# First norm and attention projection in one stage by quarters, and attention unrolled with fewer instructions a head

## The reference, cut to what matters

```python
h = rms_norm(x, g_mix)                    # x: 2048 tokens x 1024
proj = h @ w_in                           # 1792 columns for the recurrence, 512 q, 128 k, 128 v
q, k = rms_norm over 64 dims of each head (q_gain, k_gain)      # 8 q heads, 2 kv heads
s = q @ k.T * 64 ** -0.5                  # each block of 128 queries against 384 keys
s = where(valid, s + bias, -inf)          # bias by distance, |distance| <= 128
m = maximum(max(s), sink)                 # one sink logit a head
pr = exp(s - m)
o = (pr / (sum(pr) + exp(sink - m))) @ v
x = x + concat(rwkv(proj), o) @ w_out
x = x + conv_glu(rms_norm(x, g_ffn))
```

## Time and profile before

| | |
|---|---|
| median of 3 runs | 3601.62 us (3600.74 to 3607.77) |
| the profiled execution | 3603.11 us, of which span 3601.3 us |
| PE busy | 3110.9 us, 86% of the span |
| DVE, ACT, POOL busy | 1673.6, 1176.5, 473.4 us |
| mean granted TensorE clock | 0.94 |

### The profile page before, as it was taken

How to read it: one execution, slowest core, us unless ns; L and a number is a source line. 1 busy time by engine, 2 the same in 40 slices (tenths; PEclk the granted TensorE clock), 3 DMA queues, 4 the chain that set the end, 5 groups by cost and what they waited for, 6 DMA issues and landing times. The chain is left out here.

```text
span 3601.3 us, 66272 instructions
## 1 busy us (share of the span) xinstructions
PE 3110.9 (86%) x27436; PEld 2532.8 (70%) x27436; DVE 1673.6 (46%) x2214; ACT 1176.5 (33%) x2240; POOL 473.4 (13%) x724
## 2 busy tenths in 40 slices
PE   3797888997562999999469859999999999799999
PEld 1575666886332999899237638888888888688887
DVE  3666773333454555543455564444444444333333
ACT  3335552112442444444233332222222222122222
POOL 0000000000326666561310000000000000000000
PEclk7899999998785999999789979999999999899999
DMA  4000002322355333321743101111111111522231
GB/s 121 24 12 27 15 15 62 70 70 66 115 217 176 103 108 113 101 62 33 225 154 117 70 18 47 47 52 47 47 47 47 47 47 47 199 90 82 93 96 35
DMA packets 185054, 284.69 MB, mean 79 GB/s; under 512 B 60009, under 2 KB 126953, under 8 KB 180234
## 3 DMA queue, kind: packets, MB, share of 16 engines
q1 hardware_dynamic: 183402, 280.41, 24.0%
q10 hardware_dynamic: 1440, 1.18, 0.1%
HBM read 185.09 MB, written 96.47 MB: 78 GB/s over the span
## 5 line engine op out<-in xcount | busy, mean ns | idle before, releaser
L164 PE MATMUL up_p<-h_hi,up_w_hi 128*128 128x512 f32 x1408 | 548.6, 390 | 26.6 <-DVE up_w_lo L1851 26.6
L165 PE MATMUL up_p<-h_lo,up_w_hi 128*128 128x512 f32 x1408 | 548.4, 390 | 0.0
L166 PE MATMUL up_p<-h_hi,up_w_lo 128*128 128x512 f32 x1408 | 548.4, 390 | 0.0
L1838 ACT COPY up_raw<-up_p 128x512 f32<-128x512 f32 x176 | 103.3, 587 | 718.6 <-PE up_p L166 718.6
L164 PEld LDWEIGHTS up_p<-h_hi,up_w_hi 128*128 128x128 f32 x1408 | 264.8, 188 | 82.5 <-issue 27.4
L1866 DVE TENSOR_SCALAR up_con<-up_raw,vecs_sb 128x2048 f32<-128x2048 f32 x44 | 59.3, 1347 | 539.7 <-ACT up_raw L1838 539.7
L165 PEld LDWEIGHTS up_p<-h_lo,up_w_hi 128*128 128x128 f32 x1408 | 264.7, 188 | 55.2
L166 PEld LDWEIGHTS up_p<-h_hi,up_w_lo 128*128 128x128 f32 x1408 | 264.7, 188 | 54.9
L164 PE MATMUL down_p<-down_act_hi,down_w_hi 128*128 128x512 f32 x704 | 274.7, 390 | 23.5 <-DVE down_act_lo L1991 23.5
L165 PE MATMUL down_p<-down_act_lo,down_w_hi 128*128 128x512 f32 x704 | 274.6, 390 | 0.0
L166 PE MATMUL down_p<-down_act_hi,down_w_lo 128*128 128x512 f32 x704 | 274.5, 390 | 0.0
(11 more groups left out here) (230 smaller groups left out, 6476.7 us busy)
## 6 DMA issues: line engine op xcount, KB each, us to landing
rec_inp<-gate_chunks SPq DMA_DIRECT2D x64, 512.0 KB, 3.5
up_w<-in_w_up SPq DMA_DIRECT2D x44, 512.0 KB, 3.4
act_out<-up_con SPq DMA_DIRECT2D x22, 1024.0 KB, 4.3
down_act<-act_out SPq DMA_DIRECT2D x88, 256.0 KB, 3.2
gate_chunks<-gates_out SPq DMA_DIRECT2D x4, 4096.0 KB, 11.9
rkv_chunks<-rwkv_project_mix SPq DMA_DIRECT2D x12, 1024.0 KB, 6.5
down_w<-in_w_down SPq DMA_DIRECT2D x22, 512.0 KB, 13.5
gate_chunks<-gates_out SPq DMA_DIRECT2D x4, 2048.0 KB, 7.1
```

Of the source, the lines that this page charges most:

```text
L164: pe.matmul(out, w_hi, x_hi, start=start, stop=False)
L165: pe.matmul(out, w_hi, x_lo, start=False, stop=False)
L166: return pe.matmul(out, w_lo, x_hi, start=False, stop=stop)
L1838: nc.scalar.copy(raw[:, half, 1 + n * NT:1 + (n + 1) * NT], p_u[:, half, n]).then_inc(S["copied_" + c], 1)
```

## The change

`start_block` and `attn_project_block` become `first_block`. It goes over 24 items g: quarter n = g // 6, column tile m = g % 6. Each item loads and splits its own weights again, 24 times instead of 6, ACT casting all 1024 columns at once and POOL subtracting. x has one buffer; the norm of quarter n + 1 is spread over the items of quarter n: squares at m = 1 and 2, root and reciprocal at m = 3, POOL's scaling in place at m = 3 and 4, high and low parts (with the gain, from the scaled tile) at m = 4 and 5. Normalised q is multiplied by -1/8 and stored to HBM (`q_dram`); k stays in SBUF. The bias row is negated, so scores and bias have their signs turned.

`attention_block` is unrolled over all 128 heads of blocks. q comes back from HBM. A score contracts the 64 rows of its kv head. One DVE instruction adds the bias and takes the minimum with the negated sink. The exponential has scale -1 and one more column, which holds the sink, so its sum is the whole denominator. POOL scales the probabilities by the reciprocal; the transposed tiles are copied by ACT and DVE in turn; weighing takes v as weights and the probabilities as moving data and writes channels on partitions, so the output transpose and the division are gone. The stages of a head lie up to 11 heads apart.

```diff
+            def _(sp):                                  # first_block
+                def load_x(n, ks):
+                    for k in ks:
+                        done(sp, "low", (n - 1) * KD + k + 1)
+                        sp.dma_start(xt[:, k], K.d["xT"][:, k, toks(n)]).then_inc(S[f"x_in{k}"], 16)
+                def load_w(g):
+                    done(sp, "w_lo", g)
+                    sp.dma_start(w[:, :, :], K.d["w_attn"][g % MT]).then_inc(S["w_in"], 16)
...
+                load_w(0)
+                sp.wait_ge(S["bias_copied"], 1)
+                sp.dma_start(K.bias_rows, row.unsqueeze(1).to_broadcast([AH, P, 512])).then_inc(
+                    S["bias_out"], 16)
+                def body(g, n, m):
+                    if g + 1 < ITEMS:
+                        load_w(g + 1)
+                    if m == 0 and n + 1 < TN:
+                        load_x(n + 1, range(KD))
+                    if m >= 1 and is_qk(g - 1) and m - 1 < QK - 1:
+                        q = g - 1
+                        done(sp, "normed", qk_count(q) + 1)
+                        sp.dma_start(K.q_dram[:, m - 1, toks(n)], raw[:, q % 2]).then_inc(
+                            S[f"q_saved{q % 2}"], 16)
+            def _(pe):
+                def body(g, n, m):
+                    done(pe, "w_lo", g + 1)
+                    done(pe, "copied", g - 1)
...
+                    for k in range(KD):
+                        if m == 0:
+                            done(pe, "low", n * KD + k + 1)
+                        mm = product(pe, p_proj[:, g % 2], w_hi[:, g % 2, k], w_lo[:, g % 2, k],
+                                     K.h_hi[:, k, toks(n)], K.h_lo[:, k, toks(n)], k == 0, k == KD - 1)
+                    mm.then_inc(S["projected"], 1)
+                    if g >= 1:
+                        heads(g - 1) if is_qk(g - 1) else turn_v(g - 1)
+                    if n + 1 < TN and m in (1, 2):
+                        squares(n + 1, range(4 * (m - 1), 4 * m))
+            def _(act):
+                def take(g):
+                    done(act, "projected", g + 1)
...
+                    if g == 0 or g == 1:
+                        done(act, "bias_out", 16)
...
+                def body(g, n, m):
+                    if g + 1 < ITEMS:
+                        split(g + 1)
+                    if g >= 1:
+                        head_root(g - 1) if is_qk(g - 1) else copy_v(g - 1)
+                    if n + 1 < TN:
+                        if m in (1, 2):
+                            squares(n + 1, range(4 * (m - 1), 4 * m))
+                        elif m == 3:
+                            root(n + 1)
+                        elif m >= 4:
+                            high(n + 1, range(4 * (m - 4), 4 * (m - 3)))
+                    take(g)
+            def _(pool):
+                def body(g, n, m):
+                    if g + 1 < ITEMS:
+                        split(g + 1)
+                    if n + 1 < TN and m in (3, 4):
+                        scale(n + 1, range(4 * (m - 3), 4 * (m - 2)))
+            def _(dve):
+                def body(g, n, m):
+                    if g >= 1 and is_qk(g - 1):
+                        normed(g - 1)
+                    if n + 1 < TN:
+                        if m == 3:
+                            invert(n + 1)
+                        elif m >= 4:
+                            low(n + 1, range(4 * (m - 4), 4 * (m - 3)))
...
+    PB = 12                                             # attention_block
+    TURN, WEIGH = 8, 10
...
+                    rows = slice(HD * (h // HH), HD * (h // HH) + HD)
+                    done(pe, "biased", i - 2)
...
-                    pe.matmul(p_s[:, h % 2, lo:hi], q_heads[:, h, :],
-                              K.qk[:, AH // 2, bass.ds(b * P - P + lo, hi - lo)], start=True,
+                    pe.matmul(p_s[:, i % 3, lo:hi], q[rows, b % 2, h % HH],
+                              K.k_t[rows, b * P - P + lo:b * P - P + hi], start=True,
...
-                        mm = pe.matmul(p_o[:, j, h % HH, :], prob_t[:, h % 2, c, :], v,
+                    out = p_o[HD * (h % 2):HD * (h % 2) + HD, b % 2, h // 2]
+                        mm = pe.matmul(out, K.v_tok[:, b - 1 + c, HD * j:HD * j + HD], prob_t[:, i % 4, c],
...
+                slots(pe, (0, score), (TURN, turn), (WEIGH, weigh))
+                    nc.scalar.activation(prob[:, i % PB, lo:hi + 1], s_sb[:, h, lo:hi + 1], ACT.Exp, scale=-1.0,
+                                         bias=least[:, b % 2, h:h + 1],
+                                         accum_out=den[:, b % 2, h:h + 1]).then_inc(S["exped"], 1)
+                slots(act, (1, exp), (TURN + 1, copy), (WEIGH + 1, copy_out))
+                    nc.gpsimd.tensor_scalar(prob[:, i % PB, lo:hi], prob[:, i % PB, lo:hi],
+                                            inv[:, b % 2, h:h + 1], None, ALU.mult).then_inc(S["scaled"], 1)
+                slots(pool, (5, scale))
+                    nc.vector.tensor_tensor_reduce(
+                        s_sb[:, h, lo:hi], p_s[:, i % 3, lo:hi], bias[:, h, lo:hi], 1.0, nsink[:, h:h + 1],
+                        ALU.add, ALU.min, least[:, b % 2, h:h + 1]).then_inc(S["biased"], 1)
+                slots(dve, (0, score), (2, invert), (TURN + 1, copy))
```

More of the change, by code:

```diff
@@ L204, in _ @@
+                sp.dma_start(outside, K.d["outside"]).then_inc(S["rb_in"], 16)
                 sp.dma_start(relb[:, :], K.d["rel_bias"]).then_inc(S["rb_in"], 16)
[L205 to L214, removed]
@@ L217, in _, with squares @@
             @block.scalar
             def _(act):
[L219 to L228, removed]
+                def squares(n, ks):
+                    for k in ks:
+                        done(act, f"x_in{k}", 16 * (n + 1))
+                        done(act, "x_summed", n * KD + k - 1)
+                        nc.scalar.activation(sq[:, k % 2], xt[:, k], ACT.Square).then_inc(S["x_squared"], 1)
@@ new lines, in _ @@
+                act.wait_ge(S["const_in"], 32)
+                squares(0, range(KD))
+                root(0)
+                split(0)
+                high(0, range(KD))
+                def body(g, n, m):
[11 more added lines that the diff above has]
+                    take(g)
@@ L383, in attention_block @@
     HH = AH // 2
+    W = 3 * P
+    ITEMS = NB * AH
+    PB = 12
+    TURN, WEIGH = 8, 10
     with ExitStack() as ctx:
@@ L406, in window @@
         def window(b):
-            end = isinstance(b, int)
-            return (P if end and b == 0 else 0, 2 * P if end and b == NB - 1 else 3 * P)
-        def has(b):
-            return not isinstance(b, int) or b >= 0
-        def wait(eng, name, value):
-            if not isinstance(value, int) or value > 0:
-                eng.wait_ge(S[name], value)
-        def item(b, h):
-            return (b, h) if h >= 0 else (b - 1, h + AH)
-        def blocks(eng, body):
-            body(0)
-            body(1)
-            with eng.Fori(2, NB - 1) as b:
-                body(b)
-            body(NB - 1)
+            return (P if b == 0 else 0, 2 * P if b == NB - 1 else W)
@@ L430, in attention_block, with done, copied, slots @@
+        def done(eng, name, n):
+            if n > 0:
+                eng.wait_ge(S[name], n)
+        def copied(eng, i):
+            if i >= 0:
+                done(eng, "copied_odd" if i % 2 else "copied_even", i // 2 + 1)
+        def slots(eng, *stages):
+            last = max(lag for lag, _ in stages)
+            for i in range(ITEMS + last):
+                for lag, stage in stages:
+                    if 0 <= i - lag < ITEMS:
+                        stage(*items[i - lag])
         with nc.Block() as block:
@@ L489, in slot @@
-                def slot(b, h, scores=True):
-                    if scores:
-                        score(b, h)
-                    for lag, stage in ((2, turn), (3, weigh)):
-                        if has(item(b, h - lag)[0]) and (scores or h - lag < 0):
-                            stage(*item(b, h - lag))
-                    if h == 5 and has(b - 1):
-                        turn_out(b - 1)
-                blocks(pe, lambda b: [slot(b, h) for h in range(AH)])
-                for h in (0, 1, 2, 5):
-                    slot(NB, h, False)
+                slots(pe, (0, score), (TURN, turn), (WEIGH, weigh))
```

531 lines of the change are left out of this document (244 added, 287 removed).

## The result

The changed kernel takes **3850.2 us** (median of 4 runs, 3845.3 to 3855.8), the kernel before 3604.7 beside it (4 runs): a ratio of 1.068, 95% interval 1.066 to 1.070. It is 6.8% slower, where the forecast was 3574 in a range of 3545 to 3640. The profiled execution took 3855.8 us, its span 3854.0.

A forecast was written before the change was run, and what follows sets the result against it. A four-engine chain was taken to pace attention, PE to bound the projection. First stage +37 and attention -65 us sum to -28, giving a 3574 us median; own range 3558 to 3592, full range 3545 to 3640.

The forecast's parts named there:

- the columns streamed stay 384 and 6x128, so I leave the 1.64: Attention: PE needs 1.64 us a head without a stall, unchanged by the 64-row score and weighing.
- the 222 us of the forecast: Attention stage: entry, first scores, 200 us of PE work, draining and last store sum to 222 us against 286.8.
- Stops at shape changes: Attention: changes between 64- and 128-row shapes on PE, taken as costing nothing, 0.17 us each kept for the range.
- Rival R1: Attention: PE drains at three shape changes a head, 0.51 us a head, 65 us; kernel 3639; chance 0.15.
- a loss of 1.7 us that ends by itself: First stage: restart after a long PE wait runs at clock 0.57 over 4 us, losing 1.7 us.
- R5: Attention: the four-engine chain still sets the pace, so nothing is saved there; kernel 3639; chance 0.04.
- DVE's pass: Attention: DVE's bias addition with the minimum taken in it, 0.72 us a head, bounds 0.56 and 1.11.
- Bias DMA out: First stage, start: the 2 MB bias DMA, read from 8 partitions, goes out near 26.5 us.
- R3: First stage: weights not held behind the bias DMA, product 1 starts 36 us earlier; kernel 3538; chance 0.06.
- I add 1.8 for the 8 us idle in each of three quarters: First stage, quarters: low-clock loss after PE's 8 us idle, 1.8 us on 60.3 us a quarter.
- at the long end: First stage: DVE and GpSimd block each other over SBUF, three middle waits growing by 9 us in all, within the range.
- The store-then-load chain: First stage: weight loads wait behind q's stores, 9.4 us an item; alone paces the last quarter, 44 us from item 19.

The follow-up runs named there:

- run 3: Changed kernel with full tiles in both attention matmuls: zero-padded 128-row score and 128-column weighing (outputs overlap, left so): 3596.1 us, attention 218.5 us.
- Run 4: Changed kernel with 16 extra full matmuls ahead of the ninth head, all tile shapes as changed: 3670.8 us, attention 291.8 us.
- run 1: Changed kernel with only the score widened to 128 rows (q zero-padded), transposing and weighing as changed: 3634.9 us, attention 258.2 us.
- run 5: Changed kernel with 16 extra full matmuls ahead of the ninth head, plus 16 idle GpSimd operations before head 64's scaling: 3778.3 us, attention 403 us.
- run 8: Changed kernel with the 2 MB bias write read from 128 partitions, not 8: 3818.5 us, first stage ending at 298.0 instead of 332.0 us.
- run 9: Changed kernel with q's store one item later in SyncE's order: 3840.6 us, first stage ending at 319.5 us.
- run 10: Changed kernel with GpSimd's scaling left out in quarters 2 to 4, its wait for the reciprocal kept: 3847.9 us, first stage ending at 323.8 us.
- run 6: Changed kernel with 16 extra full matmuls at the very start of attention, ahead of the first score: 3860.7 us.
- run 7: Changed attention behind the norm and projection stages of the kernel before, with q stores added: 3802.2 us, attention 481.7 us.
- run 11: Changed kernel with both the later q store and GpSimd's scaling left out in quarters 2 to 4: 3827.9 us, first stage ending at 303.9 us.
- run 2: Changed kernel with weighing over all 128 columns of v, 64-row score kept (outputs overlap, left so): 3722.2 us, attention 341.9 us.
- run 12: Old norm and projection with q stored by DMA, 128-partition bias write, changed attention with full tiles: 3537.4 us, ratio 0.981 to the kernel before.

## Why the prediction was wrong, by its own steps

**The step that failed** is "the columns streamed stay 384 and 6x128, so I leave the 1.64". It took a head's PE time from the earlier trace rows, read at a clock of 0.98, and let it stand for other shapes at whatever clock came. Two things were missing. The sizes, for attention, from the 222 us of the forecast:
- The columns at full clock were right: 218.5 us with full tiles (run 3), -3.5. (By its own terms the 200 us of PE work are 198.)
- **Stops at shape changes**, taken as nothing: 3 x 0.16 us a head. Run 4 less its 15 us of extra matmuls gives 277 us, +58. Rival R1 had both the price (0.17) and the sum (65). The earlier trace rows was the wrong witness, as the text itself noted: no shape changes in it. The upper bound came from the nearest row of the same work, and was right. The rule that the prediction takes from the Trainium skill, "TensorEngine Tiling (Array Packing)", "Key Properties", that a change of mode drains the engine, agrees with runs 1, 3 and 4, by 0.16 us a change.
- **The clock**: 482.5 - 277 = +205 us. No rival had it. PE enters the stage at 0.50 after its wait for bias and q, and the changed mix doesn't lead out of that level, though PE is busy 100% and though it would keep the high one (runs 4 and 5). The earlier trace rows had shown low clocks after waits; I priced them as a loss of 1.7 us that ends by itself. It did end so in runs 1 and 3, some 3 us after the scores resume (346.7 in run 1), and with this mix it didn't.

**What held.** R5, the chain as pace: no, DVE, ACT and POOL trail PE. Their loads: DVE's pass 0.60 + 0.08 against 0.72, ACT's exponential and half copies 1.09 a head against 1.0, POOL's scaling 1.20 against "0.78 to 1.12", a little over the upper bound and still under PE's 1.64. The rest of the kernel: +2 us.

**First stage, start.** PE waits once for 34.7 us before product 1, ended by POOL's split (said over 30). Bias DMA out at 21.9 (said 26.5), the weights of product 1 landed at 22.8 + 44.9 = 67.7 (69.5), its end 79.0 (80.2). The mechanism is shown by run 8, and R3 is refuted. These are 34 of the 55 us, and the wide write avoids them.

**First stage, quarters.** The waits were right; the step that failed is "I add 1.8 for the 8 us idle in each of three quarters", the clock behind them. From the end of product 1 (79.0) to that of product 19 (282.8) it is 203.8 us against 3 x 62.1 = 186.3. That is 17.5 of the 18 us of the miss in this stage. Product 11 starts 16.4 us after the end of product 9 (forecast 16.5), with PE idle 7.9 us before it (forecast 8). Products 11 and 12, with the columns of the earlier trace rows, and the wait between:
```profile
185.80:194.40 8.60, 8.60 (x25) 6.86 (x26) 7.25 (x5) 1.04 (x1) 8.60 (x5) 0.64 0.28 91
```
```profile
199.89 2.43 POOL L396 TENSOR_TENSOR first_w_lo<-first_w,first_w_hi 128x1024 fp32r<-128x1024 f32 x1 [4.60 <-ACT first_w_hi L329]
202.92 0.80 PE L164 MATMUL first_p_proj<-h_hi,first_w_hi 128*128 128x512 f32 x1 [4.57 <-DVE h_lo L418]
```
```profile
202.90:208.40 5.50, 5.48 (x13) 4.21 (x14) 1.96 (x3) 0.00 (x0) 0.00 (x0) 0.50 0.74 224
```
Product 11 takes 8.6 us and not 5.45, and the second half of product 12 takes 5.5 and not 2.7: 5.9 us a quarter, 4.1 more than was added. The other 2 us are interference. The low part that PE waits for took DVE from 200.04 to 202.79, 2.75 us where one alone takes 0.68, and GpSimd's split ended at 202.32. The prediction had that at the long end, 9 us in all. So the wrong price is the same as in attention, here at 12 us: a full clock was assumed soon after a wait.

The store-then-load chain was right: from the end of product 19 to the end of the stage 49.2 us, forecast 46.8 + 0.7, and run 9 takes 14 us of that away. Scaling was priced at 1.2 us. The four tiles ahead of the split took 1.23 each, and the four behind it, beside DVE, 1.70, so the mean is 1.53. Leaving the work out gave some 3.6 us a quarter and not 8 (run 10), because the wait for the reciprocal stayed. The rule that the prediction takes from the Trainium skill's "SBUF — State Buffer", "Who interferes with whom", is borne out in both directions: GpSimd's side in the changed kernel's own rows, DVE's by run 10, at 2.5 times its time.

**The sum**: 3574 + 18 (first stage) + 58 + 205 - 4 (attention) + 2 = 3853, against the median 3850.2 and the profiled 3855.8. The range ended at 3640 because it held R1 alone, and no bound for a stage at the other clock level: 1.64 x 128 more, +210 us, could have been written down from the earlier trace rows.

**Open**: what in the mix the chip weighs. Either narrow operand can be widened to get the high level, with the score within microseconds and with the weighing only after 180 us. The number of shape changes alone doesn't decide it. Transposes in turn with 64-column weighing, two changes a head, brought the clock back within 7 us of the last score in eight traces (the changed kernel's and runs 5 to 11). The 64-row score with full weighing, two changes a head as well, took over 180 us (run 2). That points to the 64-row score, with one run on one side of the comparison.

## What to carry to other kernels

Take every PE duration together with the granted clock beside it, and when a change narrows tiles or alternates shapes, price the whole stage at both levels. Price the work behind every PE wait at the low level too. Filling the tiles (zeros beside q, the unneeded columns of v) cost no PE time here and is worth 3 x 0.16 us a head, and with it the clock came back after the wait at the entry (runs 1, 3 and 12). A DMA that expands a few rows should read from all partitions, above all when later loads stand behind it in the same queue: that was 34 us here. A DVE operation with two SBUF inputs should be priced beside GpSimd, not alone. And leaving out an engine's work says little while its wait keeps its place in the order (runs 10 and 11).

## What the runs showed of the hardware

- One instruction mix was seen at either clock level: 1.00 for over 110 us, then, after one stop of 16 us, 0.50 for 200 us (run 5). In run 6 it fell to 0.50 after a stop of 1.7 us where the mix begins. PE was 100% busy at 0.50 for 400 us (run 7).
- Each change between 64- and 128-wide tiles cost 0.16 us of PE at full clock (runs 1 to 4).
- 2 MB read from 8 partitions held about half of the DMA capacity for some 44 us (21.9 to about 66); read from 128 partitions they and the loads behind them moved at 346 GB/s (run 8).
- Beside each other, a DVE operation with two SBUF inputs went from 0.68 to 1.71 us and GpSimd's from 1.23 to 1.70 (128x512, float32). Behind a GpSimd split of 2.43 us one such DVE operation took 2.75.
